# RWKV-7 chunk scan on TensorE: all heads on the diagonal quadrants of the array, and two waits of TensorE for its own products taken out

## The reference

```python
def rwkv_scan(r, decay, k, v, kk, a, s0):
    def step(s, inp):
        rt, wt, kt, vt, kkt, at = inp
        sa = jnp.einsum('bhvk,bhk->bhv', s, -kkt)
        s = s * wt[:, :, None, :] + sa[..., None] * (kkt * at)[:, :, None, :] + vt[..., None] * kt[:, :, None, :]
        return s, jnp.einsum('bhvk,bhk->bhv', s, rt)
```

## Time and profile before

| | us |
|---|---|
| median of 3 runs (2829.07 to 2831.11) | 2829.89 |
| the profiled execution | 2832.73 |
| its span, first to last instruction | 2830.9 |
| granted TensorE clock, mean of the span | 0.949 |

### The profile page before, as it was taken

One profiled execution on the slowest core, in us unless ns is written; L12 is line 12 of the kernel. 1 busy time (PEld: TensorE's weight loads), 2 busy tenths in 40 slices (PEclk: granted clock), 3 DMA queues, 4 the chain that ended last, 5 costly groups with the idle time before them and its releaser, 6 DMA issues.

```text
span 2830.9 us, 60504 instructions
## 1 busy us (share of the span) xinstructions
PE 2588.6 (91%) x27787; PEld 1795.2 (63%) x27788; DVE 664.5 (23%) x1098; ACT 468.8 (17%) x781; POOL 46.4 (2%) x146
## 2 busy tenths in 40 slices
PE   6998878999999778868888879999999999999997
PEld 2562732444444366857788569696969696969593
DVE  1033443000000266764776420000000010100001
ACT  3232012100000143443233120000000000000000
POOL 0000002200000000000000000000000000000000
PEclk9988989999999889989999789999999999999999
DMA  6215104522222320042001248888889898979793
GB/s 242 75 60 222 61 17 193 186 74 75 74 74 81 134 67 1 4 130 89 2 4 43 81 158 317 305 319 301 324 298 328 292 334 288 339 284 343 278 347 121
DMA packets 179204, 492.95 MB, mean 174 GB/s; under 512 B 9410, under 2 KB 73236, under 8 KB 172804
## 3 DMA queue, kind: packets, MB, share of 16 engines
q1 hardware_dynamic: 177156, 482.73, 47.8%
q0 software_dynamic: 1792, 6.19, 0.7%
HBM read 487.84 MB, written 1.05 MB: 173 GB/s over the span
## 4 chain that ended last, share of the span: by engine, by line
PE 86%; DVE 8%; ACT 3%; issue 2%; DMA 2%; SPq 0%; POOL 0%; DVEq 0%; ACTq 0%; POOLq 0%
PE banks L1022 24%; PE banks L1039 14%; PE banks L604 11%; PE banks L736 11%; PE banks L805 6%; PE banks L746 5%; PE banks L646 2%; PE banks L543 1%; PE banks L996 1%; PE banks L938 1%; DVE rstd L1363 1%; PE banks L1007 1%; PE banks L698 1%; PE banks L769 1%; PE banks L780 1%
## 5 line engine op out<-in xcount | busy, mean ns | idle before, releaser
L1022 PEld LDWEIGHTS banks<-ring_arena 128*64 128x64 f32 x14336 | 687.1, 137 | 19.1 <-issue 18.2
L1022 PE MATMUL banks<-ring_arena 128*64 128x112 f32 x14336 | 694.0, 259 | 0.0
L1039 PE MATMUL banks<-ring_arena 128*112 128x512 f32 x896 | 385.8, 592 | 0.0
L604 PE MATMUL banks<-ring_arena 128*128 128x256 f32 (+1 forms) x1024 | 314.5, 470 | 22.0 <-ACT ring_arena L1078 12.7
L736 PE MATMUL banks<-ring_arena 128*128 128x512 f32 x704 | 305.0, 596 | 0.0
L1039 PEld LDWEIGHTS banks<-ring_arena 128*112 128x112 f32 x896 | 158.0, 177 | 221.9 <-issue 221.9
L604 PEld LDWEIGHTS banks<-ring_arena 128*128 128x128 f32 x1024 | 199.6, 195 | 137.4 <-issue 96.2
L1868 DVE TENSOR_TENSOR ring_arena<-ring_arena,banks 128x448 f32<-128x448 f32 x32 | 19.9, 621 | 1033.1 <-PE banks L1022 1033.1
L736 PEld LDWEIGHTS banks<-ring_arena 128*128 128x128 f32 x704 | 134.7, 192 | 169.6 <-issue 169.6
L805 PE MATMUL banks<-ring_arena 64*64 64x128 f32 (+1 forms) x6144 | 203.3, 258 | 29.0 <-DVE ring_arena L1679 15.1
L805 PEld LDWEIGHTS banks<-ring_arena 64*64 64x64 f32 x6144 | 190.9, 137 | 36.2 <-issue 20.5
(11 more groups left out here) (293 smaller groups left out, 1847.4 us busy)
## 6 DMA issues: line engine op xcount, KB each, us to landing
ring_arena<-in_moe_w_gu SPq DMA_DIRECT2D x256, 896.0 KB, 5.5
ring_arena<-in_moe_w_d SPq DMA_DIRECT2D x112, 1024.0 KB, 7.1
ring_arena<-in_mod_w SPq DMA_DIRECT2D x48, 1024.0 KB, 7.4
ring_arena<-in_ff_w_gu SPq DMA_DIRECT2D x22, 1024.0 KB, 5.1
ring_arena<-in_rw_w_rkv SPq DMA_DIRECT2D x20, 1024.0 KB, 10.9
ring_arena<-in_gla_w_in SPq DMA_DIRECT2D x12, 1024.0 KB, 5.4
ring_arena<-in_ff_w_d SPq DMA_DIRECT2D x11, 1024.0 KB, 4.9
ring_arena<-in_gla_w_out SPq DMA_DIRECT2D x4, 1024.0 KB, 13.8
```

What stands on the lines that cost most here:

```text
L604: ins = T.matmul(b[:, 0:width], w[:, k, j * P:j * P + P], src[:, k, :], start=(k == 0), stop=(k == KT - 1))
L1022: ins = T.matmul(bank[CH * h:CH * h + CH, (c % 4) * CAP:(c % 4) * CAP + CAP], w[:, kk, c * P + CH * h:c * P + CH * h + CH], XG[:, 2 * kp + ...
L1039: ins = T.matmul(ps[6 + h][0:CAP, :], HX[:, 2 * u + k, :], w[:, k, 512 * h:512 * h + 512], start=(u == 0 and k == 0), stop=(u == WD_UNITS ...
```

## The change

The parameter `cross` goes, and every call of `heads` works on the straight quadrants. The two waits of TensorE on `pe_s`, ahead of W and ahead of V·Mrk, go too. Number, order, shapes and operands of the matmuls are the same, as are all programs of the other engines.

```diff
-            def heads(d, half, lhs, rhs, cross, first=True, last=True):
+            def heads(d, half, lhs, rhs, first=True, last=True):
                 bank = scan_banks(d, half)
                 for p in range(HP):
                     for r in range(2):
                         x = rhs[rows[r], p, :]
-                        ins = T.matmul(bank[rows[1 - r if cross and p >= HP // 2 else r], p, 0:x.shape[-1]],
+                        ins = T.matmul(bank[rows[r], p, 0:x.shape[-1]],
                                        lhs[rows[r], p, :], x, start=first and p % (HP // 2) == 0, stop=last,
                                        skip_group_check=True)
                 return ins
...
                 levels(3)
                 for d in range(2):
-                    pe.wait_ge(pe_s[d], PES.value(lat, i, "LakV"))
-                    heads(d, 1, AI[d][:, :, 0:CH], w[d]["ST"], True, first=False).then_inc(pe_s[d], 1)
+                    heads(d, 1, AI[d][:, :, 0:CH], w[d]["ST"], first=False).then_inc(pe_s[d], 1)
...
                     for d in range(2):
-                        pe.wait_ge(pe_s[d], PES.value(lat, i, "y0"))
-                        heads(d, 1, V[d], w[d]["Mrk"], True, first=False, last=False)
-                        heads(d, 1, w[d]["SA"], w[d]["Mrb"], True, first=False).then_inc(pe_s[d], 1)
+                        heads(d, 1, V[d], w[d]["Mrk"], first=False, last=False)
+                        heads(d, 1, w[d]["SA"], w[d]["Mrb"], first=False).then_inc(pe_s[d], 1)
```

More of the change, by code:

```diff
@@ L811, in raw @@
                 pe.wait_ge(fr_s[d], FRS.value(g // SC, g % SC, "A"))
-                heads(d, 0, pick(AA[d], d, g), WORK[d][f"AI{g % 2}"], True).then_inc(raw_pe[d], 1)
+                heads(d, 0, pick(AA[d], d, g), WORK[d][f"AI{g % 2}"]).then_inc(raw_pe[d], 1)
             def level(d, lat, i, l):
@@ L818, in level @@
                     pe.wait_ge(bt_act[d], SC * lat + i + 1)
-                    heads(d, 0, w["SL"], w["Z0"], True).then_inc(lv_s[d], 1)
+                    heads(d, 0, w["SL"], w["Z0"]).then_inc(lv_s[d], 1)
                 elif l < 5:
@@ L822, in level @@
                     pe.wait_ge(za_s[d], ZAS.value(lat, i, f"C{l - 1}"))
-                    heads(d, 0, w["SL"], w["ZT"], True).then_inc(lv_s[d], 1)
+                    heads(d, 0, w["SL"], w["ZT"]).then_inc(lv_s[d], 1)
                 else:
@@ L829, in level @@
                         pe.wait_ge(dv_s[d], DVS.value(lat, i, "Mrk"))
-                    heads(d, 1, w["S5"], w["ZT"][:, :, CH:2 * CH], True).then_inc(lv_s[d], 1)
+                    heads(d, 1, w["S5"], w["ZT"][:, :, CH:2 * CH]).then_inc(lv_s[d], 1)
             def scan(lat, i):
@@ L844, in scan @@
                     pe.wait_ge(dv_s[d], DVS.before(lat, i))
-                    heads(d, 1, KX[d], AI[d], True).then_inc(pe_s[d], 1)
+                    heads(d, 1, KX[d], AI[d]).then_inc(pe_s[d], 1)
                 levels(1)
@@ L849, in scan @@
                         pe.wait_ge(dv_s[d], DVS.value(lat, i, "Lak"))
-                        heads(d, 1, VT[:, i if d == 0 else SC - 1 - i], EYES, True).then_inc(S["vt"], 1)
+                        heads(d, 1, VT[:, i if d == 0 else SC - 1 - i], EYES).then_inc(S["vt"], 1)
                 if lat:
@@ L856, in scan @@
                         pe.wait_ge(fr_s[d], FRS.value(lat, i, "R"))
-                        heads(d, 1, pick(AA[d], d, g), w[d]["R"], True).then_inc(pe_s[d], 1)
+                        heads(d, 1, pick(AA[d], d, g), w[d]["R"]).then_inc(pe_s[d], 1)
                 levels(2)
@@ L861, in scan @@
                     pe.wait_ge(dv_s[d], DVS.value(lat, i, "Mrb" if lat else "Lak"))
-                    heads(d, 1, w[d]["Lak"], V[d], False, last=False).then_inc(pe_s[d], 1)
+                    heads(d, 1, w[d]["Lak"], V[d], last=False).then_inc(pe_s[d], 1)
                 levels(3)
                 for d in range(2):
-                    pe.wait_ge(pe_s[d], PES.value(lat, i, "LakV"))
-                    heads(d, 1, AI[d][:, :, 0:CH], w[d]["ST"], True, first=False).then_inc(pe_s[d], 1)
+                    heads(d, 1, AI[d][:, :, 0:CH], w[d]["ST"], first=False).then_inc(pe_s[d], 1)
                 levels(4)
@@ L870, in scan @@
                         pe.wait_ge(ac_s[d], ACS.value(lat, i, "W"))
-                        heads(d, 1, KX[d], w[d]["R"], True).then_inc(pe_s[d], 1)
+                        heads(d, 1, KX[d], w[d]["R"]).then_inc(pe_s[d], 1)
                 levels(5)
@@ L877, in scan @@
                     pe.wait_ge(za_s[d], ZAS.value(lat, i, "C5"))
-                    heads(d, 1, w[d]["TT6"], w[d]["W"], False).then_inc(pe_s[d], 1)
+                    heads(d, 1, w[d]["TT6"], w[d]["W"]).then_inc(pe_s[d], 1)
                 if lat:
@@ L881, in scan @@
                         pe.wait_ge(ac_s[d], ACS.value(lat, i, "SA"))
-                        heads(d, 1, w[d]["ST"], w[d]["R"], False, last=False).then_inc(pe_s[d], 1)
+                        heads(d, 1, w[d]["ST"], w[d]["R"], last=False).then_inc(pe_s[d], 1)
                     for d in range(2):
-                        pe.wait_ge(pe_s[d], PES.value(lat, i, "y0"))
-                        heads(d, 1, V[d], w[d]["Mrk"], True, first=False, last=False)
-                        heads(d, 1, w[d]["SA"], w[d]["Mrb"], True, first=False).then_inc(pe_s[d], 1)
+                        heads(d, 1, V[d], w[d]["Mrk"], first=False, last=False)
+                        heads(d, 1, w[d]["SA"], w[d]["Mrb"], first=False).then_inc(pe_s[d], 1)
                 for d in range(2):
@@ L891, in scan @@
                         pe.wait_ge(ac_s[d], ACS.value(lat, i, "SA"))
-                    heads(d, 1, w[d]["Kt"], V[d], True, last=False)
-                    heads(d, 1, w[d][f"Bt{g % 2}"], w[d]["SA"], True, first=False).then_inc(pe_s[d], 1)
+                    heads(d, 1, w[d]["Kt"], V[d], last=False)
+                    heads(d, 1, w[d][f"Bt{g % 2}"], w[d]["SA"], first=False).then_inc(pe_s[d], 1)
             for sg in range(2):
```

## The result

The changed kernel takes 2906.0 us (median of 4 runs, 2900.79 to 2908.29) against 2829.55 us: 2.6% slower, ratio 1.0263 with a 95% interval of 1.0248 to 1.0278. The profiled execution took 2906.66 us. The forecast was 2906 us.

The account below looks back on a forecast made before the run. TensorE's array pace and the chain of waits through VectorE and ScalarE were both taken to bound the scans; context +36 and latent +40 gave +76 us on 2829.89, so 2906 us, range 2888 to 2926.

Parts of the forecast that it names:

- What a call costs: Calls of `heads` in the scans: straight 1.74 us for 128 columns, 0.93 for 64; crossed 1.00 and 0.59.
- The context stages: Five stages of each context-scan chunk: +8.8 us in chunks 1 to 3, about +9.5 in the fourth, +36 us.
- The latent stages: Latent-scan chunks: +11.6 us each, four times; after deductions, including half-clock costs and issue pauses, +40 us.
- The pauses put down to issue: TensorE's 5.5 us of scan pauses that nothing in the profile releases: partly covered after the change, half taken, -2.7 us.
- The clock: Five falls to 0.50 in the scans: most go as the pause ahead of Kt·V shrinks to 1.2 us; +8.3 if all stay.
- The sum: Context and latent scans together: 36 + 40 = +76 us, giving 2906 us, 2.7% slower.
- The waits: TensorE's two given-up waits, ahead of W and V·Mrk: costed at nothing.
- A clock that stays low: Rival: half an array counts as idle, clock at 1.2 GHz for much of the scans: +165 us, 3071 us; chance 0.04.
- The pace is the issuing: Rival: issuing, not the quadrant, sets the pace; straight calls keep 1.00 and 0.59 us: 2818 us; chance 0.02.
- what works on the same rows is done one after the other: Rival: quadrants sharing rows work in turn, so crossing bought nothing and the time stays at 2830 us; chance 0.02.

Follow-up runs that it names:

- the filled pause: Kernel before with TT6·W issued twice for each direction in all chunks but the last of each segment: 2835.0 us, ratio 1.0005.
- one half after the other: Changed kernel with loops turned round, each call doing all 8 products on rows 0 to 63, then 8 on rows 64 to 127: 3402.79 us, ratio 1.201.
- alternation: Kernel before with issue order alternating straight and crossed quadrants: by pairs 2819.33 us, ratio 0.9959; by blocks of two pairs 2815.25 us, ratio 0.9935.

## Why the prediction was right

- **What a call costs.** Right in each number: 1.75 us a straight 128-column call (1.74), 0.93 for 64 columns (0.93), with the pair times read from the kernel before.
- **The context stages.** 8.79 us for the second context chunk (8.8), the stages within 0.06 us of the forecast; in the whole scan +34.9 (36).
- **The latent stages.** Right in sum, +38.9 (40). A chunk with VT grew by 10.1 us, where 11.6 stood less the pauses put down to issue, of which 2.2 us went there. The next, without VT and with a fall of the clock in it before, grew by 9.0, where 11.6 less 1.3 stood and another 0.9 of pauses went.
- **The pauses put down to issue.** They stood at -2.7 us, the middle of 0 and 5.5. All seven lay in the latent scan, and there they shrank to 1.0 us: -4.5. (The 4.7 us of the changed kernel's profile hold 3.7 in the context scan; its four of 0.6 us are the stop ahead of L5 of the second direction, which the profile before puts down to VectorE, 0.69 us each.) That nothing in the profile releases them was wrong for 3.6 of the 5.5 us: they end 0.10 us behind the copy of V.
- **The clock.** The pause shrank to 1.05 us (1.2) and the falls went. That they went because it shrank is not shown: with the levels alone straight it kept its 2.18 us and they went all the same. Their price was a little high: 1.3 us each by the pace of calls, 1.1 of array time by the filled pause.
- **The sum.** +76 was forecast for the scans and +73.8 came; the 2 us are about what the pauses gave beyond their -2.7.
- **The waits.** Right: put back, they cost nothing.
- **The rivals.** A clock that stays low didn't come with half the array at work. It did with a quarter, behind a pause (one half after the other), so the 0.04 for this rival was not too much. "The pace is the issuing" is ruled out by alternation, "what works on the same rows is done one after the other" by the change itself, which cost time, and by alternation, which gained some. The Trainium skill's rule (TensorE: Matmul & The Clock Gate, Part 3), that weight loads overlap only products of another row group, is not what this trace shows: calls whose straight and crossed quadrants share rows take 0.46 us with their weight loads, on straight quadrants alone 0.93. The Trainium skill's TensorEngine Tiling, Tiling Modes, says that different tiles load and multiply in parallel, and the traces agree: alternating by one or two pairs reaches the factor of two (0.46 against 0.93 us for 64 columns, 0.87 against 1.75 for 128). In blocks of four pairs, as in the kernel before, it is less (0.59 and 1.00).

## What to carry to other kernels

Small products on the array are streams, one for each quadrant, and the time is that of the fullest stream, as long as the next ones are issued close enough: alternate the quadrants every pair or two, not in long blocks. A wait of an engine for its own product cost nothing here, where another product was still running; read what runs at that moment before giving anything up for it. And a pause that the profile puts down to issue may be a wait: look at what ended 0.1 us before it.

## What I had not expected of the hardware

- With one quadrant at work the granted clock stayed at 1.00 for 110 us until a pause of 1.40 us; behind it, it was 0.50 and stayed there, in the latent scan for 535 us without idle time. With two quadrants it stays at 1.00 through 149.55 busy of 160 us.
- The look-ahead past a busy quadrant, in the two kernels in which it was read, is three records of that quadrant, not a number of instructions in all.
- Filling a pause with useless products kept the clock whole (1.00 where it was 0.50) and still gained nothing that can be measured in the time. The same pause with longer calls before it brought no fall either.
